# Processing the experts of a mixture layer in an order computed on the chip

## What is computed

```python
logits = (xt @ w_router + b_router)          # 256 tokens x 32 experts
top_logits, top_idx = lax.top_k(logits, 4)
top_w = jax.nn.softmax(top_logits, axis=-1)
...
def expert_block(args):                      # for each expert e, on its tokens
    gate, up = jnp.split(xb @ w_gu[e] + b_gu[e], 2, axis=-1)
    ...
    act = (up + 1) * (gate * jax.nn.sigmoid(SWIGLU_ALPHA * gate))
    return act @ w_dn[e] + b_dn[e]
```

## Time and profile before

| | |
|---|---|
| median of 3 runs | 2322.34 us (2320.06 to 2329.26) |
| the profiled execution | 2318.49 us |
| its span, first to last instruction | 2316.6 us |
| PE busy | 2165.1 us (93%) |
| mean granted TensorE clock | 0.983 |
| moved by DMA | 591.31 MB, mean 255 GB/s |
| the loop over experts, first to last copy of a down result | 417.15 to 1421.54 us |

### The profile page before, as it was taken

The page is one execution under the profiler, slowest core; times in us unless marked ns, Lnnn a source line. Parts: engine busy times, 40 slices in busy tenths (PEclk is TensorE's granted clock), DMA queues, the critical chain, the costliest instruction groups (busy, mean ns, idle before and its releaser), DMA issues.

```text
span 2316.6 us, 30267 instructions
## 1 busy us (share of the span) xinstructions
PE 2165.1 (93%) x11523; PEld 1138.8 (49%) x11524; DVE 751.5 (32%) x1836; ACT 468.7 (20%) x930; POOL 65.4 (3%) x79
## 2 busy tenths in 40 slices
PE   5999998989999998999989998999999999999998
PEld 4844455343333333333333334844565446787873
DVE  1596234212222222222211223232212353988100
ACT  1011102111111111111110111131112215898100
POOL 0000000000000000000000000000000000222000
PEclk9999998999999999999999999999999999999999
DMA  9645557859999999999996799435133323232241
GB/s 345 223 163 181 209 196 285 337 224 417 418 418 418 418 418 381 418 417 418 417 383 265 317 417 384 148 112 200 68 141 133 123 103 125 74 110 74 103 164 42
DMA packets 158855, 591.31 MB, mean 255 GB/s; under 512 B 5323, under 2 KB 6927, under 8 KB 125887
## 3 DMA queue, kind: packets, MB, share of 16 engines
q1 hardware_dynamic: 152512, 573.08, 63.2%
q0 software_dynamic: 4384, 16.40, 2.0%
q10 hardware_dynamic: 1887, 0.81, 0.1%
HBM read 589.23 MB, written 1.05 MB: 255 GB/s over the span
## 4 chain that ended last, share of the span: by engine, by line
PE 74%; DMA 15%; DVE 5%; ACT 3%; DVEq 2%; issue 1%; ACTq 0%; SPq 0%
PE PS L616 22%; PE PS L922 13%; DMA W<-in_w_gu 13%; PE PS L604 10%; PE PS L945 6%; PE PS L1129 4%; PE PS L631 4%; PE PS L869 2%; PE PS L958 2%; PE PS L1202 1%; DVE BIG L1924 1%; PE PS L886 1%; DVE BIG L1928 1%; DMA W<-in_w_mod 1%; DVEq L1927 1%
## 5 line engine op out<-in xcount | busy, mean ns | idle before, releaser
L616 PE MATMUL PS<-W,BIG 128*128 128x512 f32 x1152 | 501.0, 596 | 5.0 <-DVE BIG L2358 2.9
L922 PE MATMUL PS<-W,BIG 128*64 128x512 f32 x2048 | 451.8, 595 | 21.0 <-DMA W<-in_w_gu 20.9
L616 PEld LDWEIGHTS PS<-W,BIG 128*128 128x128 f32 x1152 | 219.4, 191 | 277.2 <-issue 270.5
L922 PEld LDWEIGHTS PS<-W,BIG 128*64 128x64 f32 x2048 | 142.1, 137 | 313.0 <-issue 270.8
L945 PE MATMUL PS<-W,BIG 128*64 128x512 f32 x1024 | 228.8, 600 | 7.0 <-ACT BIG L1408 6.9
L604 PE MATMUL PS<-BIG,W 128*128 128x256 f32 x1024 | 222.2, 379 | 1.4 <-ACT BIG L354 1.4
L604 PEld LDWEIGHTS PS<-BIG,W 128*128 128x128 f32 x1024 | 194.2, 190 | 28.9 <-ACT BIG L354 1.9
L1922 DVE TENSOR_SCALAR BIG<-PS 128x512 f32<-128x512 f32 (+1 forms) x38 | 24.7, 650 | 379.6 <-PE PS L922 355.9
L945 PEld LDWEIGHTS PS<-W,BIG 128*64 128x64 f32 x1024 | 71.1, 138 | 144.0 <-issue 126.3
L1403 ACT ACTIVATE BIG<-BIG 128x512 f32<-128x512 f32 x32 | 20.2, 632 | 488.9 <-DVE BIG L1922 488.9
L1129 PE MATMUL PS<-BIG,W 128*128 128x256 f32 x512 | 118.3, 385 | 0.5 <-ACT BIG L1563 0.5
(11 more groups left out here) (460 smaller groups left out, 1963.2 us busy)
## 6 DMA issues: line engine op xcount, KB each, us to landing
W<-in_w_gu SPq DMA_DIRECT2D x128, 2048.0 KB, 17.3
W<-in_w_dn SPq DMA_DIRECT2D x64, 2048.0 KB, 19.1
W<-in_w_in SPq DMA_DIRECT2D x24, 2048.0 KB, 15.1
W<-in_w_mod SPq DMA_DIRECT2D x12, 2048.0 KB, 9.6
W<-in_gla_w_in SPq DMA_DIRECT2D x10, 2048.0 KB, 7.9
W<-in_s_w_in SPq DMA_DIRECT2D x8, 2048.0 KB, 8.9
W<-in_s_w_glu SPq DMA_DIRECT2D x8, 2048.0 KB, 8.0
W<-in_w_out SPq DMA_DIRECT2D x6, 2048.0 KB, 8.3
```

The source lines that it names most:

```text
L616: ins = pe.matmul(ps[:, t, :], lhs(i * KT + k)[:, t * P:(t + 1) * P], w[:, k, :], start=i + k == 0, stop=last_chunk and k == KT - 1)
L922: ins = pe.matmul(PS[hh[h], g, :], XET[:, k, :], gu_w(k)[:, g * D + h * CH:g * D + (h + 1) * CH], start=False, stop=k == KT - 1, skip_grou ...
```

## The change

The experts are taken in another order, which is the same computation but for the order of the sums. The loop index is now a position, and a table `PERM` gives the expert at it. Expert 0 stays at position 0. The others are ranked by their token count, the highest count first (ties by index), and the expert of rank r goes to the position whose 5-bit number is r with its bits reversed: rank 1 to position 16, rank 2 to 8, rank 3 to 24, rank 4 to 4, rank 5 to 20, rank 6 to 12, rank 7 to 28, rank 8 to 2 and so on, the odd positions last.

PE counts each expert's tokens once more, one expert to a partition (`OWN_COUNT`). DVE compares all counts, sums the comparisons to a rank and makes a 32x32 permutation matrix `ORDER`. PE multiplies the counts and the expert numbers with it, DVE copies the numbers to `PERM`, and the tables are computed from the placed counts. SP reads one register from `PERM` for each expert that it loads, DVE one for each expert and one more for each that has extra blocks.

```diff
@@ constants()
+    own = -np.arange(NE, dtype=np.float32)
+    own[0] = 4 * T * NE
+    c[:, C_TIE:C_TIE + NE] = own
+    c[0:NE, C_OWN] = own
+    c[0:NE, C_OWN + 1] = np.arange(NE)
+    spread = sorted(range(NE), key=lambda i: int(f"{i:05b}"[::-1], 2))
+    c[:, C_PLACE + np.array(spread)] = np.arange(NE)
@@ SP
                     def load_expert(e, previous):
-                        gu = A["w_gu"][0, bass.ds(e, 1)].rearrange("e (k p) n -> p (e k) n", p=P)
-                        dn = A["w_dn"][0, bass.ds(e, 1)].rearrange("e (k p) n -> p (e k) n", p=P)
+                        source = e if previous is None else sp.value_load(PERM[0:1, bass.ds(e, 1)], min_val=0, max_val=NE - 1)
+                        gu = A["w_gu"][0, bass.ds(source, 1)].rearrange("e (k p) n -> p (e k) n", p=P)
+                        dn = A["w_dn"][0, bass.ds(source, 1)].rearrange("e (k p) n -> p (e k) n", p=P)
@@ PE
+            for t in range(TT):
+                pe.matmul(OWN_COUNT, SEL[:, t, :], ONES[:, 0:1], start=t == 0, stop=t == TT - 1)
...
             gather_rows(0, True)
+            pe.wait_ge(ev("sel_ready"), 2)
+            pe.matmul(PLACED_COUNT, RANK[:, 0:1], ORDER, start=True, stop=True)
+            pe.matmul(PLACED_EXPERT, K[0:NE, C_OWN + 1:C_OWN + 2], ORDER, start=True, stop=True).then_inc(ev("pos_done"), 1)
             pe.wait_ge(ev("wmt_ready"), 1)
@@ DVE
+            def placed(e):
+                return dve.value_load(PERM[0:1, bass.ds(e, 1)], min_val=0, max_val=NE - 1)
+
             def extras(e):
                 lo = dve.value_load(TABI[0:1, 0, bass.ds(e, 1)], min_val=0, max_val=64)
                 hi = dve.value_load(TABI[0:1, 1, bass.ds(e, 1)], min_val=0, max_val=64)
                 with dve.If(hi - lo > 0):
+                    own = placed(e)
                     with dve.Fori(lo, hi) as x:
-                        extra_block(x, e, nc.s_assert_within(x - lo + 1, 1, XMAX))
+                        extra_block(x, own, nc.s_assert_within(x - lo + 1, 1, XMAX))
 
             def expert(e, last):
                 if not last:
-                    one_hot(e + 1, K[:, C_SLOT:C_SLOT + BLK], PW, G, GW, ev("g_ready"))
+                    following = placed(e + 1)
+                    one_hot(following, K[:, C_SLOT:C_SLOT + BLK], PW, G, GW, ev("g_ready"))
...
                 if not last:
-                    columns_of(e + 1)
-                    one_hot_extra(e + 1, 0)
+                    columns_of(e + 1, following)
+                    one_hot_extra(following, 0)
...
             one_hot(0, K[:, C_SLOT:C_SLOT + BLK], PW, G, GW, ev("g_ready"))
-            cnt, nx = pos[0:1, 2, :], TABF[:, 0, :]
+            dve.tensor_copy(RANK[:, 0:1], OWN_COUNT)
+            dve.scalar_tensor_tensor(KEY, pos[0:NE, 2, :], float(NE), K[0:NE, C_TIE:C_TIE + NE], ALU.mult, ALU.add)
+            dve.scalar_tensor_tensor(RANK[:, 1:2], OWN_COUNT, float(NE), K[0:NE, C_OWN:C_OWN + 1], ALU.mult, ALU.add)
+            dve.drain()
+            dve.tensor_scalar(ABOVE, KEY, RANK[:, 1:2], None, ALU.is_gt)
+            dve.drain()
+            dve.tensor_tensor_scan(KEY, ONES[0:NE, 0:NE], ABOVE, 0.0, ALU.mult, ALU.add)
+            dve.drain()
+            dve.tensor_scalar(ORDER, K[0:NE, C_PLACE:C_PLACE + NE], KEY[:, NE - 1:NE], None, ALU.is_equal)
+            dve.drain()
+            dve.sem_inc(ev("sel_ready"), 1)
+            dve.wait_ge(ev("pos_done"), 2)
+            dve.tensor_copy(PERM, PLACED_EXPERT)
+            cnt, nx = PLACED_COUNT, TABF[:, 0, :]
             dve.tensor_scalar(nx, cnt, float(BLK), None, ALU.is_gt)
```

More of the change, by code:

```diff
@@ L51 @@
 C_N = C_T + T
+C_TIE = C_SLOT + P + (XMAX + 1) * XBLK
+C_PLACE = C_TIE + NE
+C_OWN = C_PLACE + NE
 R_C, R_AV, R_AG, R_CB, R_BS = 0, 8, 16, 24, 32
@@ L356, in copy_columns @@
                                ACT.Copy).then_inc(tp_copied, 1)
+        PERM = BIG[0:1, 7 * ROW + D + 968:7 * ROW + D + 968 + NE].bitcast(I32)
         TABX = MISC[0:1, 2 * P:2 * P + 6 * NE].rearrange("p (j e) -> p j e", j=6).bitcast(I32)
@@ L463, in build @@
         TABI = BIG[0:1, E7 + 896:E7 + 896 + 2 * NE].rearrange("p (a e) -> p a e", a=2).bitcast(I32)
+        RANK = BIG[0:NE, E7 + 1000:E7 + 1002]
+        KEY, ABOVE, ORDER = OH[0:NE, 0, :], OH[0:NE, 1, :], LG[0:NE, 0, :]
+        OWN_COUNT, PLACED_COUNT, PLACED_EXPERT = PS[0:NE, 2, 0:1], PS[0:1, 2, NE:2 * NE], PS[0:1, 2, 2 * NE:3 * NE]
         WMT = BIG[0:NE, 8 * ROW:8 * ROW + T].rearrange("p (t s) -> p t s", t=TT)
@@ L1905, in one_hot_extra, with columns_of @@
                         K[:, C_SLOT + P + j * XBLK:C_SLOT + P + (j + 1) * XBLK], PWX, GX, GWX, ev("x_g_ready"))
-            def columns_of(e):
-                dve.tensor_copy(SELB[0:NE], ident[0:NE, bass.ds(e, 1)].to_broadcast([NE, BLK]))
-                dve.tensor_copy(SELB[NE:2 * NE], ident[NE:2 * NE, bass.ds(e + NE, 1)].to_broadcast([NE, BLK])) \
+            def columns_of(e, own):
+                dve.tensor_copy(SELB[0:NE], ident[0:NE, bass.ds(own, 1)].to_broadcast([NE, BLK]))
+                dve.tensor_copy(SELB[NE:2 * NE], ident[NE:2 * NE, bass.ds(own + NE, 1)].to_broadcast([NE, BLK])) \
                     .then_inc(ev("selb_ready"), 1)
@@ L1977, in _ @@
             dve.sem_inc(ev("table_ready"), 1)
-            columns_of(0)
+            columns_of(0, 0)
             one_hot_extra(0, 0)
```

## The result

The median is 2308.33 us (five runs, 2304.48 to 2310.85); before it is 2320.31 (five runs by now). The ratio on record is 0.9941, its 95% interval 0.9923 to 0.9959: about 0.6% faster (the medians alone give 0.9948). The forecast was 2308, its range 2299 to 2319. A second set of four runs of the same kernel, on another occasion, had a median of 2305.84, ratio 0.9934 [0.9917, 0.9951].

What follows compares the result with a forecast made beforehand. Experts were bound by transfers and PE by turns, with 26.4 us of stalls from order alone. Order -18.7, DVE's load +3.5 and start +0.9 sum to -14.3: span 2302.3, execution 2304.2, plus 3.9 for the median, 2308; range 2299 to 2319.

Steps and rivals of the forecast that it cites:

- The store of time: Expert stage: the ring's lead lasts five ordinary experts; the new order cuts stalls from 26.4 to 7.7 us, -18.7 us.
- list of signs: ACT's timeline: five intervals near 47, one near 64.5, at positions 4, 8, 16, 20, 24; 27.79 elsewhere, 30.1 at 15.
- stalls of 26 and 8 us: Expert stage: PE's waits for gate chunks fall from 26 us in all to about 8.
- e25: Expert 25 in the old order, one extra block, 48.68 us: stalls 2.34 us, yet said to refill a full store.
- e26: Expert 26 in the old order, with an extra block, 47.79 us: said to refill a store that is full already.
- e27: Expert 27 in the old order, with an extra block, 47.79 us: said to refill a store that is full already.
- The register load behind the SwiGLU: DVE, experts with extra blocks: one more load wholly on the path, 0.7 us once per expert, +3.5 us.
- The covered loads: DVE's load at each turn's head and SP's per expert cost nothing; SP's at most 1.4 us, DVE's uncovered 21.7.
- The start: Before the first gate matmul: added counts +0.4 us and two placing matmuls +0.5, together +0.9, bounds 0 and 4.
- the clock takes some of it back: Rival, extra blocks: PE's granted clock drops; if all six blocks meet it, 5.8 us more, 2314; chance 0.17.
- Instruction loading: Rival, extra-block branches: misses cost 4.3 us per expert, 21.4 together, 2329; chance 0.05, shared with an uncovered load per expert.

Runs made afterwards that it cites:

- the repeat: The changed kernel run once more, unaltered, on another occasion: median 2305.84 us (2303.24 to 2308.56).
- even runs: Changed kernel with experts with extra blocks at positions 5, 10, 15, 21, 26, no ordinary run longer than five: 2299.10 us, ratio 0.9916 to the kernel before.
- hidden_triple: Changed kernel with two more register loads per expert on DVE at each turn's head and two on SP before transfers: 2305.17 us, ratio 0.9932 to kernel before.
- own_triple: Changed kernel with the register load in front of an extra block done three times: 2317.19 us, ratio 0.9982 to the kernel before.

## Why the prediction was right, point by point

**The time.** The mechanism held term by term, but that the median fell within 0.4 us of 2308 is luck. The forecast started from 2322.34, the median of three runs before; with five it is 2320.31. The gain of 14.3 us that I summed measured 12.0 by these medians, 13.7 by the ratio and 15.5 in the second set. The profiled execution, forecast at 2304.2, took 2310.85, and the 3.9 us by which the median stood above it before did not carry over: now the median stands 2.5 below. The stage itself adds up in both profiles. In the first, the order -18.7, the loads +3.6, the clock +2.2 (three drops, 5.1 us, for the 2.9 before) and the last expert +0.4 give the measured -12.5; in the repeat, with two drops, +0.5 for the clock and nothing for the last expert, they give -14.6.

**The store of time.** The forecast's largest term, -18.7 us, is confirmed by four placements. Stalls now: 0.31 at position 14, 2.33 at 15, 2.33 inside position 16's 68.57 (46.34 + 0.72 + 17.49 + 2.33 = 66.88, the other 1.69 is the clock), 0.39 at position 30, and 2.33 within position 31. Sum 7.7, as forecast. With the old order they are 26.4, with the heavy experts first about 47, with even runs 0. Three details of my text were off, and the sum did not use them. I gave position 16 as near 64.5 in the list of signs, though my own sum has it stall 2.33: it is 66.88 without the clock. I took the stalls of 26 and 8 us for PE's recorded waits, which are 20.9 and 5.8. And e25 did not refill a full store, since it stalled 2.34 itself; only e26 and e27 did.

**The register load behind the SwiGLU.** Forecast 0.7 each, 3.5 in all; the wait grew by 0.74 and the interval by 0.72. For this term I had set the 0.30 us of the load itself against the floor of about 0.6 us in the Trainium skill ("DMA: Bandwidth & Descriptors", latency and other measured facts) and found no agreement. The sum itself went by 0.7 us, the spacing of the two loads there, and the 0.74 bears it out. The comparison with the page was a poor one. What further loads cost on the path here, 0.61 us each with their register work, agrees with the page; 0.30 is only the record of one of the instructions.

**The covered loads.** On DVE and on SP they cost nothing, and two more of each cost nothing either.

**The start.** Forecast +0.9, of which +0.4 for the added counts and +0.5 for the two placing matmuls; in the trace at full clock they add 0.3 and 0.2. From the first position matmul (L799 before, L814 after) to the first gate matmul it is 12.46 us before and 12.98 to 13.09 in seven of the eleven profiles with the new start: +0.6. In three others, the changed kernel's first among them, it is 16.1 to 16.3, with the clock at 0.50 over the stretch; in one 14.8. So the term was sized well for one clock, but the start can cost 3.7 us, and my text looked for the clock only in the extra blocks. One thing goes with it in all eleven: in the four that lost clock PE had waited 0.67 to 0.87 us just ahead of the first position matmul, and in the seven others 0.51 or less. No run changed that pause alone, so the cause stays open. The arrival at this place shifts by some 4 us between executions (372.2 to 376.7 for that first matmul).

**The clock.** The rival "the clock takes some of it back" did act, more in one execution than in the other: three drops of 1.7 us in one profile, two in the repeat, and in the first the half clock at the start besides. Filling the pauses removes the drops in the extra blocks, but it doesn't pay.

**The last expert.** Its 33.95 us is 27.79 + 2.33 + 3.8; before it was 31.24, so 3.45 above the ordinary, and in the repeat it is 3.48 again. The 0.4 is small, but its pause ahead of the transposes changed kind: 3.09 us for DVE before, 4.0 us for nothing named after. All profiles in which the last expert waits for chunks have 3.9 or 4.0 there, the three others without fills, whose chunks are in time, have 3.1. Why is open.

**Instruction loading.** PE's gap in expert 0 stayed, 3.6 to 4.4 us once, and no branch into or out of an extra block shows another: 46.32 us for such an expert standing alone. The rule of the Trainium skill ("Runtime: NRT & Kernel Launch", instruction fetch mechanics), that a taken branch can stall for a fetch, would fit that one gap, though no run tests what the gap is; it did not bring the loss that this rival drew from it.

## What to carry to other kernels

When transfers and compute bind by turns, read the interval of each unit of work, not the share over the stage. Two numbers (compute's own interval, the transfer-bound interval) and the number of units that pass between a long one and the first stall give the size of the store, and with it the time of other orders of the work: here it gave three of them to within 3 us. Long units refill a store that has a ceiling, so spread them so that no run between them outlasts it; bit-reversed placement leaves runs of seven where the store lasts five. Put register loads for run-time indices ahead of a long wait, for behind the last computation before a hand-over they are on the path whole: 3.6 us for five of them here, and nothing for 62.

## What the runs showed of the hardware

- The sequencer of DVE reads registers while DVE computes (L1942 starts at 1230.0, during the multiplication that began at 1229.92), so a load can be free (62 at the head of the turns, `hidden_triple`) or cost 0.6 to 0.74 us (behind the SwiGLU, `own_triple`) by its place alone.
- The mean granted clock was 0.57 over the 4 us behind 4 us in which PE was busy 1.41 with small matmuls, and that at position 4 in one execution of the changed kernel and not in the other. No single wait of PE there was longer than 1.34 us. With waits of 2.56 us all five such experts lost clock, with filled pauses none did. Runs of one kernel differ by 2 to 14 us, and the faster ones mostly have the higher mean clock (0.984 at 2304.48 us, 0.980 at 2310.85).
